# Expert weights of a mixture stage laid out with neighbouring rows in each partition, in a fused float32 two-block kernel

## The reference, cut to what matters

```python
def layer_norm(x, g, b):
    mu = jnp.mean(xf, -1, keepdims=True); var = jnp.mean(jnp.square(xf - mu), -1, keepdims=True)
    return ((xf - mu) * lax.rsqrt(var + LN_EPS)).astype(x.dtype) * g + b

def routed_moe(x, router_w, router_b, w_gate, w_up, w_down):
    aff = jax.nn.sigmoid((xt @ router_w).astype(jnp.float32))
    ...                                   # two experts of one group of four for each token
    for e in range(N_EXPERTS):            # 16 experts, D = 1024, inner width 512
        h = jax.nn.silu(xt @ w_gate[e]) * (xt @ w_up[e])
        y = y + gates[:, e:e + 1] * (h @ w_down[e])
```

## Time and profile before

| | us |
|---|---|
| median of 3 runs (2489.87 to 2492.24) | 2491.63 |
| the profiled execution | 2491.5 |
| its span | 2489.7 |
| PE busy in the span | 2263.9 (91%) |
| DVE busy | 1737.1 (70%) |
| ACT busy | 1176.1 (47%) |

### The profile page before, as it was taken

One profiled execution on the slowest core, in us unless ns is written; L12 is line 12 of the kernel. 1 busy time (PEld: TensorE's weight loads), 2 busy tenths in 40 slices (PEclk: granted clock), 3 DMA queues, 4 the chain that ended last, 5 costly groups with the idle time before them and its releaser, 6 DMA issues.

```text
span 2489.7 us, 33608 instructions
## 1 busy us (share of the span) xinstructions
PE 2263.9 (91%) x13722; PEld 2001.3 (80%) x13722; DVE 1737.1 (70%) x2087; ACT 1176.1 (47%) x1344; POOL 243.6 (10%) x184
## 2 busy tenths in 40 slices
PE   7779999997679899997999988899989989888997
PEld 7667788887467788886998977689989988767997
DVE  4667579995657578996776686677767766476554
ACT  3544356873443346784334663343343344434333
POOL 5102002312002001310000022000000020000000
PEclk9889999998889999998999998999999999998999
DMA  8136679993125678995876322478768734305651
GB/s 241 51 124 243 233 258 331 358 361 134 51 73 186 245 253 326 357 356 167 305 265 210 137 85 85 146 253 275 239 208 290 264 124 146 119 1 177 203 181 56
DMA packets 241433, 505.55 MB, mean 203 GB/s; under 512 B 10367, under 2 KB 104513, under 8 KB 241280
## 3 DMA queue, kind: packets, MB, share of 16 engines
q1 hardware_dynamic: 216128, 417.84, 47.8%
q10 hardware_dynamic: 21600, 77.09, 8.8%
q0 software_dynamic: 3552, 8.47, 1.5%
HBM read 502.31 MB, written 1.05 MB: 202 GB/s over the span
## 4 chain that ended last, share of the span: by engine, by line
PE 43%; DVE 7%; ACT 3%; issue 1%; ACTq 0%; DVEq 0%
PE PS L1049 21%; PE PS L1064 10%; PE PS L892 5%; PE PS L850 3%; DVE WGL L2192 1%; DVE AR L2195 1%; DVE X L2192 1%; DVE XN L2192 1%; ACT WGH L1664 1%; PE PS L1470 1%; PE PS L1087 1%; DVE AR L2192 0%; PE PS L1099 0%; DVE XTB L2192 0%; DVE XN L2189 0%
## 5 line engine op out<-in xcount | busy, mean ns | idle before, releaser
L2192 DVE TENSOR_TENSOR WGL<-ring,WGH 128x2048 fp32r<-128x2048 f32 x258 | 598.7, 2327 | 251.2 <-ACT WGH L1664 143.2
L1049 PE MATMUL PS<-XTB,WGH 128*128 128x256 f32 x2816 | 517.2, 285 | 6.8 <-DVE XTB L2192 6.6
L1049 PEld LDWEIGHTS PS<-XTB,WGH 128*128 128x128 f32 x2816 | 448.4, 193 | 17.5 <-issue 10.0
L1049 PE MATMUL PS<-XTB,WGL 128*128 128x256 f32 x1408 | 400.5, 284 | 0.0
L1049 PEld LDWEIGHTS PS<-XTB,WGL 128*128 128x128 f32 x1408 | 272.1, 193 | 0.0
L2192 DVE TENSOR_TENSOR WDL<-ring,WDH 128x1024 fp32r<-128x1024 f32 (+1 forms) x136 | 221.4, 1628 | 35.5 <-ACT WDH L1818 23.1
L892 PE MATMUL PS<-XTB,WGH 128*128 128x256 f32 (+1 forms) x1104 | 214.1, 295 | 29.2 <-DVE WGL L2192 25.8
L1818 ACT ACTIVATE WGH<-ring 128x2048 fp32r<-128x2048 f32 x96 | 183.2, 1913 | 121.4 <-PE PS L1120 73.3
L1664 ACT ACTIVATE WGH<-ring 128x2048 fp32r<-128x2048 f32 (+1 forms) x74 | 138.6, 1877 | 177.0 <-PE PS L892 58.7
L892 PEld LDWEIGHTS PS<-XTB,WGH 128*128 128x128 f32 (+1 forms) x1104 | 177.7, 197 | 42.3 <-DVE WGL L2192 28.4
L1857 ACT ACTIVATE XN<-PS 128x256 f32<-128x256 f32 x88 | 33.9, 385 | 356.8 <-PE PS L1049 326.0
(11 more groups left out here) (490 smaller groups left out, 4527.5 us busy)
## 6 DMA issues: line engine op xcount, KB each, us to landing
FA<-in_ada_w ACTq DMA_DIRECT2D x144, 512.0 KB, 6.0
ring<-in_moe_w_up SPq DMA_DIRECT2D x64, 1024.0 KB, 7.2
ring<-in_moe_w_gate SPq DMA_DIRECT2D x64, 1024.0 KB, 7.9
ring<-in_moe_w_down SPq DMA_DIRECT2D x64, 1024.0 KB, 7.2
ring<-in_ffn_w_gate SPq DMA_DIRECT2D x44, 1024.0 KB, 5.6
ring<-in_ffn_w_up SPq DMA_DIRECT2D x44, 1024.0 KB, 9.2
ring<-in_ffn_w_down SPq DMA_DIRECT2D x44, 1024.0 KB, 7.3
ring<-in_hyb_w_in SPq DMA_DIRECT2D x10, 1152.0 KB, 6.7
```

What stands on the lines that cost most here:

```text
L1049: ins = mm(PS[:, 4 + b, m * T:(m + 1) * T], w_[:, b, w], x_[:, k, :], start=k == 0 and q == 0, stop=k == KD - 1 and q == 2)
L2192: return V.tensor_tensor(out_, x_, y_, op)
```

## The change

The rows of the mixture's weights are given to the partitions in runs. Partition p of `w_up` and `w_gate` gets the rows 8p to 8p + 7, and a piece holds four neighbours of them; partition p of `w_down` gets the rows 4p to 4p + 3, a piece two of them. Each partition's part of a piece is then one run of 8 KB. Row tile k now stands for the positions k, k + 8, k + 16, ... of the token, and k, k + 4, k + 8, ... of the inner vector, so the stationary operands of `trn` (in the mixtures), `gathered`, `turned` and `folded` step through SBUF by 8 or 4 numbers, that is 32 or 16 bytes. `RW` is loaded in the same order. The gain and offset of the normalisation ahead of a mixture come from a new tile `LNP`, loaded by four more DMAs on POOL's queue, and ACT waits for `later_load` before it uses them. The numbers of matmuls, weight loads and vector instructions, and their sizes, stay.

```diff
-        src = w_down[e].rearrange("a (c p) n -> p (a c) n", p=P)[:, 2 * h:2 * h + 2, :]
+        src = w_down[e].rearrange("a (p c) n -> p (a c) n", p=P)[:, 2 * h:2 * h + 2, :]
...
-        src = (w_up if what == "up" else w_gate)[e].rearrange("a (k p) n -> p (a k) n", p=P)
+        src = (w_up if what == "up" else w_gate)[e].rearrange("a (p k) n -> p (a k) n", p=P)
...
-        N_SMALL, N_LATER, N_ROWS, N_FOLD = 7, 23, [0], 10
+        N_SMALL, N_LATER, N_ROWS, N_FOLD = 7, 27, [0], 10
...
-            ld(RW[:, :, :], a["router_w"].rearrange("(k p) e -> p k e", p=P), "later_load")
+            ld(RW[:, :, :], a["router_w"].rearrange("(p k) e -> p k e", p=P), "later_load")
+            for l in range(2):
+                for m, w in enumerate(("ln_g", "ln_b")):
+                    ld(LNP[:, l, m, :], a[w][l, 0].rearrange("(p k) -> p k", p=P), "later_load")
...
+            def strided(row, n, k):
+                return row.rearrange("p (q k) -> p k q", k=n)[:, k, :]
...
+                            k = 2 * j + i
+                            ins = nc.tensor.transpose(
+                                PS[:, 4 + j, i * T + t * P:i * T + (t + 1) * P],
+                                strided(src[:, t, :], KD, k) if by_partition else src[:, t, k * P:(k + 1) * P], ID)
...
-                            ins = mm(PS[:, 4, (4 * m + c) * 64:(4 * m + c + 1) * 64], UE[:, m, c * P:(c + 1) * P], FOLD,
+                            ins = mm(PS[:, 4, (4 * m + c) * 64:(4 * m + c + 1) * 64], strided(UE[:, m, :], 4, c), FOLD,
...
-                        ins = nc.tensor.transpose(PS[:, 4 + t, c * P:(c + 1) * P], HM[:, u % 2, c * P:(c + 1) * P], ID)
+                        ins = nc.tensor.transpose(PS[:, 4 + t, c * P:(c + 1) * P], strided(HM[:, u % 2, :], 4, c), ID)
...
-                            ins = mm(PS[:, 6 + k // 4, (k % 4) * P:(k % 4 + 1) * P], X[:, j, k * P:(k + 1) * P],
+                            ins = mm(PS[:, 6 + k // 4, (k % 4) * P:(k % 4 + 1) * P], strided(X[:, j, :], KD, k),
...
+                    elif norm and r.kind == "moe":
+                        f(XT[:, k, :], src, ACT.Identity, scale=LNP[:, r.layer, 0, k:k + 1],
+                          bias=LNP[:, r.layer, 1, k:k + 1]).then_inc(S("xt"), 1)
...
+                act.wait_ge(S("later_load"), 16 * N_LATER)
                 trn_out(r, r.u, norm=True)
```

More of the change, by code:

```diff
@@ L291, in program @@
         SINK = sb("SINK", [P, 8])
+        LNP = sb("LNP", [P, 2, 2, KD])
         SSDD = sb("SSDD", [P, 8])
@@ L820, in columns, with trn @@
                       .then_inc(S("cols_ps"), 1)
-            def trn(u, src):
+            def strided(row, n, k):
+                return row.rearrange("p (q k) -> p k q", k=n)[:, k, :]
+            def trn(u, src, by_partition=False):
                 if u == 0:
@@ L829, in trn @@
                         for i in range(2):
-                            ins = nc.tensor.transpose(PS[:, 4 + j, i * T + t * P:i * T + (t + 1) * P],
-                                                      src[:, t, (2 * j + i) * P:(2 * j + i + 1) * P], ID)
+                            k = 2 * j + i
+                            ins = nc.tensor.transpose(
+                                PS[:, 4 + j, i * T + t * P:i * T + (t + 1) * P],
+                                strided(src[:, t, :], KD, k) if by_partition else src[:, t, k * P:(k + 1) * P], ID)
                         if t == TT - 1:
@@ L1306, in slot_read @@
                         pe.wait_ge(S("m_route"), 5 * r.me + 5)
-                trn(r.u, X)
+                trn(r.u, X, True)
                 pe.wait_ge(S("xt"), 8 * (r.u + 1))
```

## The result

| | before | after |
|---|---|---|
| median | 2490.75 us (4 runs, 2489.43 to 2492.24) | 2594.18 us (4 runs, 2591.06 to 2597.21) |
| ratio | | 1.0415, 95% interval 1.0397 to 1.0433 |
| the profiled execution | 2491.5 us | 2591.06 us |
| its span | 2489.7 us | 2589.3 us |

The changed kernel is slower by 103.4 us at the median and by 99.6 us between the two profiled executions. The forecast of no change is wrong, and the time lies above the range too. Rival 2, loads at half rate, came nearest with 2601 us, though two of its four groups of loads did not slow the kernel as it said.

The account below looks back on a forecast made before the run. PE, busy throughout the mixtures at full clock, was taken as the bound. From the profiled 2491.5 us, transfers, stepped loads and small edits each added 0, giving 2491 us; the 8-in-10 range was 2484 to 2557 us.

Parts of the forecast that it names:

- Rival 2: PE's stepped weight loads in all four groups of loads run at half rate: +109.7 us, 2601 us; chance 0.15.
- four groups of loads: Stepped loads on PE: gathers 59.8 us, folds 30.2, turned inner vectors 12.4, tokens at a mixture's start 7.3; sum 109.7.
- What bounds the kernel: In the mixtures PE, at full granted clock, sets the end; transfers arrive ahead of their use.
- The transfers: 192 expert weight pieces in 8 KB runs: hidden, counted 0; gain on the `ada_w` side between 0 and 7.7 us.
- The strided weight loads: PE's loads stepping 32 or 16 bytes: cost between 0 and +109.7 us, taken as 0.
- Small edits: POOL's four more DMAs, `RW`'s 128 runs, ACT's new wait, scale and bias from another tile: all 0.
- Rival 1: PE's stepped loads slowed by a part: +22 to +66 us, at the middle +44, 2535 us; chance 0.20.
- Rivals 3 and 4: At `ada_w`: 3, bigger runs crowd it out, +14 us, chance 0.10; 4, rank waits vanish, up to -7.7 us, 0.12.

## Why the prediction was wrong, point by point

- **What bounds the kernel** was right, and so was the price of a load on it. PE's busy time rose by 102.1 us and the time by 103.4; gathers and folds reached the end one for one.
- **The transfers** were right to be counted at nothing. They are quicker and nobody waited for them; alone the layout gives +3.5 us where the bounds were -7.7 to 0. The time moved a little the other way, which no term of the sum had.
- **The strided weight loads** are the step that failed, at the choice within it. The bounds, 0 and +109.7 us, held the truth at +94.8 us (the steps alone), but I took 0. The reason given was POOL's instruction on line 718 as the nearest row: another engine, at 2.9 ns a number, whose own pace can hide a slower read. PE takes 128 columns in 0.117 us, 0.9 ns a column, and touches 16 bytes in about 3.7 ns; with every column in a group of its own it would need 0.9 ns a group, and gets one in 1.9. A row from an engine three times slower could not show this limit. The prediction held better evidence and passed over it: the folds' pace equal to the gathers' said that the load sets it and that nothing hides a longer one, so the bound of half rate stood open for these 768 loads. The rule of the Trainium skill that it cites ("Advanced Engine Details and Errata", section "SBUF Cachelines") puts all 896 on the wrong side.
- **The size by group.** At half rate, the gathers' term was 59.8 us and is 64.5; the folds' 30.2 and 29.3. The turned vectors' 12.4 came out at about 1 us, and the tokens' 7.3 at nothing (in moe1, 3.68 us for 3.68 at the same clock). The sum of 109.7 was near the truth for the two that count, and 19 us too high for the two groups of transposes, one at full clock and one at half.
- **Small edits**: the kernel with the steps alone holds all of them, and its +94.8 us is what gathers, folds and turned vectors give by the timelines (64.5 + 29.3 + 1.1 = 94.9). They cost nothing that shows. That the two agree to 0.1 us is luck: in that kernel's profiled execution PE is busy 99.9 us longer and idle 3.2 us less.
- **Rivals.** Rival 2 is what happened to the gathers and folds, with its signs (gathers 7.8 us for the 7.5 it named, folds 3.7 for 3.8, mixtures longer, PE as busy). It had a chance of 0.15, and the range stopped short of it. That its 2601 us is within 7 us of the measured time is partly luck: it had 18.6 us too much for the transposes, and nothing for the 8.8 us under "Left over". Rival 1's middle, some loads slowed by a part, occurs only at a step of 12 bytes. Rivals 3 and 4 are out by the layout alone: PE's wait for the ranks after the change is 2.6 us in moe0, as before:

```profile
PE PS L1130 <- DVE XN L2747: 2.6, 1, 2.6
```

- **Left over.** Of the 102.1 us that PE is busy longer, 63.1 are the gathers', 29.2 the folds' and 1.0 the transposes'; 8.8 us lie on lines whose operands nobody changed. In the mixtures the granted clock is lower than before in some stretches. These are the windows of before and then of after, from about expert 4 on, in moe0 and in moe1:

```profile
320.00:552.00 232.00, 231.17 (x1258) 199.32 (x1257) 207.58 (x148) 167.42 (x129) 48.21 (x20) 1.00 0.90 327
880.00:1120.00 240.00, 238.55 (x1290) 205.33 (x1289) 211.52 (x152) 168.85 (x131) 48.82 (x20) 1.00 0.90 324
```

```profile
320.00:600.00 280.00, 277.77 (x1246) 246.08 (x1246) 207.18 (x147) 164.83 (x127) 42.45 (x20) 0.98 0.75 269
940.00:1220.00 280.00, 278.20 (x1255) 246.68 (x1254) 208.81 (x148) 164.51 (x128) 42.02 (x20) 0.99 0.75 271
```

From 385 to 388 us, for instance, it is 0.50, though PE was busy 20.00 of 20 us from 380 to 400, and two products of 512 columns take 1.06 us there for 0.62. As an estimate, 0.02 x 280 + 0.01 x 280 is some 8 us of lost clock, about the 8.8. Why the clock falls there was not isolated.

## What to carry to other kernels

Before you change a layout so that transfers get longer runs, find the operand that has to follow it, and keep two or more of its numbers in each 16 bytes where PE reads it: at 8 bytes' step the gathers took 5% longer, at 16 and more twice the time. A load with a long product ahead of it can hide most of a longer load (0.018 us of 0.12 came through with 512 moving columns), the two-pass float32 matmuls with 128 or 64 columns hid none, and a moving side stepped by 16 bytes took twice the time, all of it at the end. And when no row shows a price, do not borrow the mildest bound from a slower engine: look whether anything hides the cost, and where nothing does, give the upper bound its weight in the forecast and in the range.

## What the runs showed of the hardware

- A float32 weight load of 128 columns in PE's two-pass matmuls takes 0.117, 0.123, 0.179, 0.238 and 0.243 us at steps of 4, 8, 12, 16 and 32 bytes.
- The load of a transpose grows by only half as much at 16 bytes (140 to 209 ns, medians) as that of a two-pass matmul (191 to 327 ns, means, the folds), and eight transposes take 1.11 us for 1.03. Why they pay less a column stayed open.
- At a granted clock of 0.50 a step of 32 bytes cost the transposes nothing (3.68 us for 3.68 in moe1).
- A float32r product of 512 moving columns takes 0.46 us for 0.23 when these columns lie 16 bytes apart.
- Runs of 8 KB for 2 and 4 KB cut SP's packets by 27% (216128 to 158784), and the time these took on the engines by 1% (47.8% to 47.3% of the span).
- ACT copies 512 numbers a partition out of PSUM in 578 ns, and in 1095 ns when it writes neighbouring ones 512 bytes apart.
